# The gated feed-forward of a four-layer trunk: another order of the seven products of a pair, with three of them accumulating in one bank

## What is computed

```python
def swiglu(h, w_gate_up, w_down):
    g, u = jnp.split(h @ w_gate_up, 2, axis=-1)
    return (jax.nn.silu(g) * u) @ w_down

x = x + swiglu(rmsnorm(x, ffn_norm[i]), ffn_w_gate_up[i], ffn_w_down[i])
```

## Time and profile before

| | us |
|---|---|
| median of three runs | 2333.09 |
| lowest and highest | 2332.84 and 2336.01 |
| the profiled execution, its time | 2334.71 |
| its span, first to last instruction | 2332.9 |
| PE busy in it | 2321.0 |
| DVE busy in it | 1681.5 |
| ACT busy in it | 1109.8 |
| mean granted share of PE's clock | 0.999 |

### The profile page before, as it was taken

The page is one execution under the profiler, slowest core; times in us unless marked ns, Lnnn a source line. Parts: engine busy times, 40 slices in busy tenths (PEclk is TensorE's granted clock), DMA queues, the critical chain, the costliest instruction groups (busy, mean ns, idle before and its releaser), DMA issues. The chain is left out here.

```text
span 2332.9 us, 36910 instructions
## 1 busy us (share of the span) xinstructions
PE 2321.0 (99%) x14072; PEld 2070.6 (89%) x14072; DVE 1681.5 (72%) x2727; ACT 1109.8 (48%) x1856; POOL 310.0 (13%) x305
## 2 busy tenths in 40 slices
PE   9999999999999999999999999999999999999998
PEld 7899988899988888899988889998889998889897
DVE  8667769586965677677787858696756775959593
ACT  6268744353543344354533434454326783435353
POOL 2211140000030120000123000003320114000003
PEclk9999999999999999999999999999999999999999
DMA  4810023233323233333223323332470003233322
GB/s 161 227 55 2 2 69 103 93 107 109 109 91 109 91 109 101 98 109 107 92 92 100 118 91 109 103 103 95 124 209 28 2 2 99 73 109 109 109 91 90
DMA packets 64681, 221.52 MB, mean 95 GB/s; under 512 B 7680, under 2 KB 7808, under 8 KB 64512
## 3 DMA queue, kind: packets, MB, share of 16 engines
q1 hardware_dynamic: 58320, 208.59, 27.7%
q0 software_dynamic: 5184, 8.40, 1.7%
q10 hardware_dynamic: 1008, 2.21, 0.3%
HBM read 208.68 MB, written 2.10 MB: 90 GB/s over the span
## 5 line engine op out<-in xcount | busy, mean ns | idle before, releaser
L664 ACT ACTIVATE w_hi<-raw 128x1024 fp32r<-128x1024 f32 x244 | 257.1, 1054 | 325.7 <-DMA raw<-stream 241.9
L1126 DVE TENSOR_TENSOR w_lo<-raw,w_hi 128x1024 fp32r<-128x1024 f32 x241 | 311.3, 1298 | 118.6 <-ACT w_hi L664 118.3
L1871 PE MATMUL bank<-xs_hi,w_hi 128*128 128x512 f32 (+2 forms) x840 | 326.4, 389 | 1.4 <-DVE xs_lo L1134 0.9
L1871 PE MATMUL bank<-xs_lo,w_hi 128*128 128x512 f32 (+2 forms) x840 | 320.8, 382 | 0.0
L1871 PE MATMUL bank<-xs_hi,w_lo 128*128 128x512 f32 (+1 forms) x824 | 314.9, 382 | 0.0
L1193 DVE TENSOR_TENSOR x<-bank,x 128x512 f32<-128x512 f32 (+1 forms) x128 | 88.5, 691 | 272.5 <-PE bank L1871 272.5
L1871 PE MATMUL bank<-hid_hi,w_hi 128*128 128x512 f32 x720 | 280.5, 390 | 0.7 <-DVE hid_lo L1372 0.7
L1871 PE MATMUL bank<-hid_lo,w_hi 128*128 128x512 f32 x720 | 280.3, 389 | 0.0
L1871 PE MATMUL bank<-hid_hi,w_lo 128*128 128x512 f32 x720 | 280.1, 389 | 0.0
L1871 PE MATMUL bank<-mix_hi,w_hi 128*128 128x256 f32 (+1 forms) x704 | 228.0, 324 | 0.0
L1871 PE MATMUL bank<-mix_hi,w_lo 128*128 128x256 f32 (+1 forms) x704 | 226.5, 322 | 0.0
(11 more groups left out here) (280 smaller groups left out, 5551.6 us busy)
## 6 DMA issues: line engine op xcount, KB each, us to landing
raw<-stream SPq DMA_DIRECT2D x243, 512.0 KB, 3.6
raw_b<-pairs SPq DMA_DIRECT2D x72, 512.0 KB, 4.8
raw_a<-pairs SPq DMA_DIRECT2D x56, 512.0 KB, 4.6
w_f<-stream SPq DMA_DIRECT2D x18, 512.0 KB, 3.7
hid_hi<-mix_hi POOLq DMA_DIRECT2D x32, 128.0 KB, 4.3
hid_lo<-mix_hi POOLq DMA_DIRECT2D x32, 128.0 KB, 3.7
out<-big SPq DMA_DIRECT2D x8, 256.0 KB, 2.8
x<-x_in ACTq DMA_DIRECT2D x4, 256.0 KB, 6.6
```

The lines of the kernel that those rows point to most:

```text
L664: nc.scalar.activation(w_hi[:, slot, :], raw[:, k, :], ACT.Copy).then_inc(w_hi_ready, 1)
L1126: nc.vector.tensor_tensor(w_lo[:, slot, :], raw[:, k, :], f32(w_hi[:, slot, :]), ALU.subtract).then_inc(w_lo_ready, counted(b))
L1871: return nc.tensor.matmul(out_, w, v, start=start, stop=stop, skip_group_check=onto)
```

## The change

The seven products of a pair come in another order, a11 first, and lie in other banks. a11, s2, s3 and a22 now follow one another in bank 6 or 7, where all three accumulate on the plain product; s1 and s4 stay in bank 5, a12 is alone in bank 4. C21 is then the bank as it stands, and is read from PSUM by the product with `act_t`; C11, C12 and C22 are one addition each of two things (C11: bank 4 and the snapshot of a11; C12: bank 5 and the snapshot after s2; C22: the snapshots of s1 and after s3). The product that makes the hidden tile is cut in two halves of 256 columns, C21's first. Chunk 0 now holds the plain a11 and a12, chunks 1 and 2 the sums (s3, s1 and s2, s4), chunk 3 a22 as before. Each snapshot now has one product between the product before it and the one that waits for it.

The core of the diff; what is left out are names of semaphores in their list and the same swap of chunk numbers in `pair_high`.

```diff
-PRODUCTS = ("s1", "s2", "a11", "s4", "s3", "a12", "a22")
+PRODUCTS = ("a11", "s1", "s2", "s4", "s3", "a12", "a22")
-WEIGHT_AT = {"s3": (0, 0), "s1": (0, 512), "s2": (1, 0), "s4": (1, 512), "a11": (2, 0), "a12": (2, 512), "a22": (3, 0)}
+WEIGHT_AT = {"a11": (0, 0), "a12": (0, 512), "s3": (1, 0), "s1": (1, 512), "s2": (2, 0), "s4": (2, 512), "a22": (3, 0)}
...
                     def high(j):
+                        act.wait_ge(c21_taken, pair_at(l, p, j) + 1)
                         act.wait_ge(hid_full, t0 + j + 1)
...
-                        snap(q, 2, S1_DONE, sums_ready)
+                        snap(q, 0, A11_DONE, c11_ready)
                         if p == 0 and j == 0:
                             first_high(l, FIRST_TILES - 1)
                         if ahead:
                             pair_high(l, p, j + 1, 1)
-                            pair_high(l, p, j + 1, 2)
                         else:
                             down_high(l, p, 1)
-                        snap(q, 1, S2_DONE)
+                        snap(q, 2, S1_DONE, c22_ready)
+                        if ahead:
+                            pair_high(l, p, j + 1, 2)
+                        snap(q, 1, S2_DONE, c12_ready)
                         if ahead:
                             pair_high(l, p, j + 1, 3)
-                        snap(q, 0, A11_DONE, c21_ready)
+                        else:
+                            down_high(l, p, 2)
+                        act.wait_ge(c12_ready, q + 1)
+                        act.wait_ge(hid_lo_ready, t0 + j)
+                        nc.scalar.activation(act_t[:, H:2 * H], lin[:, 0, :], ACT.Silu).then_inc(half_silu, 1)
                         snap(q, 3, S3_DONE, c22_ready)
-                        if not ahead:
-                            down_high(l, p, 2)
-                        act.wait_ge(product_done, 7 * q + A12_DONE)
-                        act.wait_ge(hid_lo_ready, t0 + j)
-                        nc.scalar.activation(act_t[:, 0:H], bank[4][:, 0:H], ACT.Silu).then_inc(half_silu, 1)
-                        act.wait_ge(c12_ready, q + 1)
-                        nc.scalar.activation(act_t[:, H:2 * H], lin[:, 0, :], ACT.Silu).then_inc(half_silu, 1)
+                        act.wait_ge(c11_ready, q + 1)
+                        nc.scalar.activation(act_t[:, 0:H], lin[:, 1, :], ACT.Silu).then_inc(half_silu, 1)
...
                 dve.wait_ge(pair_full[j % 2], 32 * (loads_before(q) + 1))
+                if q:
+                    dve.wait_ge(sw_lo_ready, 4 * q - 1)
...
                 first_low(l, 4)
+                pair_low(l, 0, 0, 2)
                 pair_sums(l, 0, 1)
                 gate(5)
-                pair_low(l, 0, 0, 2)
                 linear(5)
...
-                        nc.vector.tensor_tensor(lin[:, 1, :], bank[6 + q % 2][:, 0:H], part_sums[:, 0, :], ALU.add
-                                                ).then_inc(c21_ready, 1)
...
-                        nc.vector.tensor_tensor(act_t[:, :], act_t[:, :], lin[:, 1:3, :].rearrange("p a t -> p (a t)"),
-                                                ALU.mult).then_inc(hid_full, 1)
+                        dve.wait_ge(half_silu, 2 * (q + 1))
+                        nc.vector.tensor_tensor(act_t[:, 0:H], act_t[:, 0:H], bank[6 + q % 2][:, 0:H], ALU.mult
+                                                ).then_inc(c21_taken, 1)
+                        dve.wait_ge(c22_ready, q + 1)
+                        nc.vector.tensor_tensor(act_t[:, H:2 * H], act_t[:, H:2 * H], lin[:, 2, :], ALU.mult
+                                                ).then_inc(hid_full, 1)
...
-                        nc.vector.tensor_tensor(lin[:, 0:3:2, :], part_sums[:, 1:3, :],
-                                                part_sums[:, 0:1, :].broadcast_to([P, 2, H]), ALU.add
-                                                ).then_inc(sums_ready, 1)
...
-                        nc.vector.tensor_tensor(lin[:, 0, :], bank[5][:, 0:H], lin[:, 0, :], ALU.add
+                        nc.vector.tensor_tensor(lin[:, 0, :], bank[5][:, 0:H], part_sums[:, 1, :], ALU.add
                                                 ).then_inc(c12_ready, 1)
...
-                        nc.vector.tensor_tensor(lin[:, 2, :], lin[:, 2, :], part_sums[:, 3, :], ALU.add
+                        nc.vector.tensor_tensor(lin[:, 2, :], part_sums[:, 3, :], part_sums[:, 2, :], ALU.add
                                                 ).then_inc(c22_ready, 1)
-                    joined(count - 1)
+                        dve.wait_ge(product_done, 7 * q + A12_DONE)
+                        if j:
+                            dve.wait_ge(half_silu, 2 * q)
+                        nc.vector.tensor_tensor(lin[:, 1, :], bank[4][:, 0:H], part_sums[:, 0, :], ALU.add
+                                                ).then_inc(c11_ready, 1)
+                    product(count - 1)
...
                     elif name == "s2":
-                        wait_past(pe, c21_ready, q - 1)
+                        pe.wait_ge(snapped, 4 * q + 1)
...
                     elif name == "s4":
-                        pe.wait_ge(snapped, 4 * q + 1)
+                        pe.wait_ge(snapped, 4 * q + 2)
...
                     elif name == "s3":
-                        pe.wait_ge(snapped, 4 * q + 2)
+                        pe.wait_ge(snapped, 4 * q + 3)
...
                     elif name == "a12":
-                        pe.wait_ge(snapped, 4 * q + 3)
+                        wait_past(pe, c11_ready, q)
```

53 lines of the change are left out of this document (25 added, 28 removed).

## The result

The changed kernel takes **2351.0 us** (median; 2350.7 to 2351.6) against 2333.5 of the kernel before on the same chip: 1.0075 times as long, 95% interval 1.0063 to 1.0087. That is 17.5 us, for which 2350.0 (2342 to 2358) had been predicted.

What follows compares the result with a forecast made beforehand. PE, busy 2321.0 of 2332.9 us, was taken to bound the kernel. Added waits less the old ones, 9.1 us in two-pair and 8.2 in seven-pair stages, together 17.3, went onto the median 2333.09: 2350.4, told as 2350, range 2342 to 2358.

Steps and rivals of the forecast that it cites:

- The old waits: PE's existing waits in the twelve two-pair and seven-pair stages: they go, 3.2 us at most.
- DVE's half microsecond: About half a microsecond of DVE saved per pair: worth nothing by itself, but pays for the longer chain through c11.
- Inner pairs: Inner pairs of seven-pair stages: a loop of 9.9 us against PE's 10.08, no wait.
- The rival in which inner pairs wait: Loop comes to 10.3 and 40 inner pairs pay 0.22 us each: 8.8 more, 2359; chance 0.08.
- The six waits: PE waits, us: two-pair s2 1.20, s4 0.23, last a22 0.78; seven-pair first a22 0.21, second s2 0.36, last a22 0.53.
- The tail: On the matmul row following a wait for a snapshot: 0.08 us extra.
- The stage terms: Net loss: two-pair stages 2.27 us times 4, 9.1; seven-pair stages 1.03 times 8, 8.2.
- The place of gate 5: DVE's gate 5 ahead of a two-pair stage: starts 0.2 us before the stage and not 3.4.
- the change is not slower: Rival: ACT comes in time to all snapshots, only the old waits go, 2329.9; chance 0.07.
- the last pairs don't wait: Rival: the third block's DMA data come early in stages' last pairs, 2342; chance 0.11, including half of those waits.
- the clock: Rival: the granted clock falls at the 8 waits of 0.86 to 1.28 us, 10 us more, 2360; chance 0.04.
- DVE from PSUM: The DVE product reading PSUM: no extra time counted; the skill's rule would add 65 ns and 0.5 us overall.

Runs made afterwards that it cites:

- experiments 9: Changed kernel with ScalarE's and VectorE's queues reordered, down blocks' high parts behind snapshots in two-pair stages' last pairs, products and additions untouched: 2330.61 us, 0.9988 of before.
- experiment 11: Kernel before, old products and additions, with seven-pair stages' second-pair sums one block earlier and two-pair stages' last first tile behind the second snapshot: 2330.72 us, 0.9988.
- experiment 5: Changed kernel with an extra VectorE addition per pair, its result unread, putting the saved half microsecond back: 2362.76 us, 1.0124 of before.
- Experiment 1: Changed kernel with gate 5 moved ahead of the third tile's low part and the next pair's sums in VectorE's queue: 2348.94 us, 1.0066 of before.
- experiment 2: Changed kernel with the third down block's high part moved behind the fourth snapshot in ScalarE's queue, last pair of a stage: 2342.12 us, 1.0038 of before.
- experiment 6: Kernel before with only the third down block's high part moved ahead of the fourth snapshot in ScalarE's last-pair queue: 2345.94 us, 1.0054 of before.
- experiment 8: Changed kernel with gate 5 first, third down block behind fourth snapshot, second-pair sums earlier, and last first tile's high half behind second snapshot: 2333.38 us, 1.0000.

## Why the prediction was right, point by point

**The bound** held: PE's stream sets the time, and the twelve stages that were named are 17.3 us longer, as the sum has it.

**What was removed.** The old waits went: at the fifth product, where they were, the changed kernel has none. And DVE's half microsecond is worth nothing by itself: experiments 9 and 11 differ in it and not in time. That it *pays* for the chain through c11 held too, experiment 5: without it each seven-pair stage loses 1.64 us more.

**Inner pairs.** Predicted: a loop of 9.9 us and no wait. The two products of DVE over the quarter read from PSUM, one pair apart:

```profile
493.33 0.42 DVE L1364 TENSOR_TENSOR act_t<-act_t,bank 128x256 f32<-128x256 f32 x1 [0.55 <-ACT act_t L836]
...
503.26 0.42 DVE L1364 TENSOR_TENSOR act_t<-act_t,bank 128x256 f32<-128x256 f32 x1 [0.55 <-ACT act_t L836]
```

9.93 us, and no wait in any inner pair. The rival in which inner pairs wait had its trigger right: at 10.39 (experiment 5) they do.

**The six waits**, predicted and measured: two-pair stage s2 1.20 and 1.19, s4 0.23 and 0.23, a22 0.78 and 0.93; seven-pair stage a22 of the first pair 0.21 and 0.125, s2 of the second 0.36 and 0.45, a22 of the last 0.53 and 0.51. The tail is 0.07 rather than 0.08. The stage terms: 9.1 and 9.5 us, 8.2 and 7.8. So the sum was met in part because two small errors of opposite sign cancel. The one of 0.15 in a22 of the two-pair stages lies in a DMA, and not in the third block's latency, which is 434.81 − 431.24 = 3.57 for the 3.64 taken. It lies in the first block's: its high part was placed 12.11 us into the stage (427.38 − 415.27), and in the four stages it starts 12.22 (the row at 427.67), 12.32, 12.46 and 12.11 in. The other three:

```profile
919.73 1.06 ACT L664 ACTIVATE w_hi<-raw 128x1024 fp32r<-128x1024 f32 x1 [1.06 <-DMA raw<-stream]
```

```profile
1372.01 1.06 ACT L664 ACTIVATE w_hi<-raw 128x1024 fp32r<-128x1024 f32 x1 [1.20 <-DMA raw<-stream]
```

```profile
2062.64 1.06 ACT L664 ACTIVATE w_hi<-raw 128x1024 fp32r<-128x1024 f32 x1 [0.84 <-DMA raw<-stream]
```

The waits ahead of a22 are 0.87, 0.99, 1.14 and 0.74, in step with it. SP issues that transfer at the same place in all four (8.54 to 8.55 in), so the spread is the transfer's own. Experiment 1 shows the same soft term from the other side: when PE arrives sooner, the data do not come as much sooner.

The first two pairs of a seven-pair stage came out closer than their two terms. The C12 addition starts 7.47 us into the stage (489.11 − 481.64) for 7.56 predicted, so a22 waits less than was said; PE then goes on in the second pair 13.59 us into the stage for 13.61, and what the first wait did not take the second one does. Together with their tails they are 0.72 for 0.73.

**The place of gate 5** was right (0.16 us before the stage for 0.2 predicted), and experiment 1 shows that it caused most of the 1.19. For s4 the walk was right; the expectation of experiment 1 took its wait for a consequence of the one ahead of s2, and that was wrong.

**The rivals.** That the change is not slower is refuted, and so is that the last pairs don't wait; experiment 2 takes these waits away by its edit and comes to 2342.1, the price put on this rival being 2342. As for the clock, the granted clock is 1.00 in the stages with waits of up to 1.19 us (the stretches above). So the rule of the Trainium skill ("TensorE: Matmul & The Clock Gate", A second HAM failure mode), by which brief idling between groups of matmuls can make the clock swing, does not show here, with three waits to a stage.

**DVE from PSUM.** The products over PSUM and over SBUF, and the addition of two SBUF parts, by groups (mean ns behind the busy time):

```profile
L1364 DVE TENSOR_TENSOR act_t<-act_t,bank 128x256 f32<-128x256 f32 x64 | 27.0, 422 | 41.0 <-ACT act_t L836 22.1 <-PE bank L1875 18.8
L1408 DVE TENSOR_TENSOR lin<-part_sums 128x256 f32<-128x256 f32 x64 | 26.9, 420 | 12.7 <-ACT part_sums L797 12.7
...
L1367 DVE TENSOR_TENSOR act_t<-act_t,lin 128x256 f32<-128x256 f32 x64 | 26.8, 419 | 0.0
```

422, 420 and 419 ns: the 65 ns that the Trainium skill ("Perfetto Trace Analysis", Optimizing Scalar/DVE Operations) would add for PSUM are not there, and leaving them out of the sum was right.

## What to carry to other kernels

When a change frees an engine that nobody waits for, ask only what it does to the order of the queues: here 32 us less of VectorE were worth nothing, and what it did to the order of the queues and the room in them cost 17.5. Walk each in-order queue at the stage's first and last pass, not only in its steady state, and look above all for an instruction that waits for a DMA or for another engine ahead of one that TensorE waits for. How much later an engine may run is what the tightest hand-over on its way has to spare, as the trace shows it, and not what the products' order suggests: 0.21 us in the second pair of the kernel before, with two products of cover, and 1.15 in experiment 11, with the same two.

## What the runs showed that was not expected

- A wait taken away returns in part elsewhere on the path: of 0.87 us won ahead of s2 (experiment 1) a22 took 0.27 back, because its data come at a time of their own. The wait on that transfer differs between stages of one execution by 0.4 us (0.74 to 1.14), in experiment 6 by 1.7 (1.22 to 2.89).
- The tail of 0.07 us on the matmul behind a wait comes also without a gap: in experiment 8 the product s3 of the first pair starts within 0.03 us of its time, and its second matmul 0.19 behind the first, where the snapshot was only just done. A hand-over just in time is not free.
- Of TensorE's 16.5 us longer span only 11.3 appear as idle time; 5.2 are counted busy, since each recorded matmul is 0.28 long at a spacing of 0.12, and the one behind a wait 0.36. Waits of this size are read from the starts, not from the busy share.
